# Tail of a decoder layer: one token tile finished on GpSimd, sums in column halves, the last tile read in halves

## The reference

```python
x = x + hybrid_mixer(rms_norm(x, norm1_w), ...)
x = x + hier_moe(rms_norm(x, norm2_w), ...)   # 32 experts, each token goes to 2
return rms_norm(x, final_norm_w)              # y * rsqrt(mean(y*y) + 1e-6) * w
```

## Time and profile before

| | us |
|---|---|
| median of 3 runs | 602.7 |
| profiled execution, its own time | 602.21 |
| span of that execution (first to last instruction) | 600.4 |
| scatter of pair 14, from its issue to its landing | 568.64 to 576.54 |
| last arithmetic instruction ends (VectorE, L2265) | 597.46 |

### The profile page before, as it was taken

The page is one execution under the profiler, slowest core; times in us unless marked ns, Lnnn a source line. Parts: engine busy times, 40 slices in busy tenths (PEclk is TensorE's granted clock), DMA queues, the critical chain, the costliest instruction groups (busy, mean ns, idle before and its releaser), DMA issues.

```text
span 600.4 us, 11954 instructions
## 1 busy us (share of the span) xinstructions
PE 573.6 (96%) x4899; PEld 441.8 (74%) x4899; DVE 252.5 (42%) x602; ACT 199.8 (33%) x429; POOL 182.9 (30%) x126
## 2 busy tenths in 40 slices
PE   8999999999999999999999999999999999987894
PEld 7978887999999888766789988656565656644541
DVE  6598534661138213465631073333222333221126
ACT  6656454723223352455525331111111211110113
POOL 3444443462557514323643202111121111210011
PEclk9999999999999999999999999999999999999998
DMA  8866543322211221004979787999999999999985
GB/s 335 330 210 194 151 146 106 105 73 73 71 38 37 72 71 37 1 2 162 408 255 411 274 320 261 396 426 426 424 426 426 426 425 424 422 427 427 413 325 221
DMA packets 32087, 152.73 MB, mean 254 GB/s; under 512 B 8759, under 2 KB 12511, under 8 KB 25376
## 3 DMA queue, kind: packets, MB, share of 16 engines
q1 hardware_dynamic: 27360, 143.77, 61.9%
q0 software_dynamic: 4528, 8.15, 3.6%
q10 hardware_dynamic: 144, 0.03, 0.0%
HBM read 143.78 MB, written 16.27 MB: 267 GB/s over the span
## 4 chain that ended last, share of the span: by engine, by line
PE 71%; DMA 19%; DVE 4%; issue 2%; POOL 1%; ACT 1%; POOLq 0%; SPq 0%; DVEq 0%; ACTq 0%
PE bank L796 32%; PE bank L843 11%; DMA xg<-h2d,tok 8%; DMA w<-in_expert_w_dram 8%; PE bank L1231 5%; PE bank L1190 4%; PE bank L1205 4%; PE bank L821 2%; PE bank L1129 2%; PE bank L1143 2%; DMA yd<-oy,dst 1%; PE bank L1123 1%; PE bank L1099 1%; PE bank L948 1%; PE bank L1015 1%
## 5 line engine op out<-in xcount | busy, mean ns | idle before, releaser
L1570 POOL TENSOR_TENSOR wlo<-raw,whi 128x1024 fp32r<-128x1024 f32 (+1 forms) x24 | 59.3, 2469 | 82.2 <-ACT whi L1260 78.8
L1697 POOL DMA_INDIRECT yd<-oy,dst x15 | 15.1, 1008 | 163.4 <-DVE oy L2226 152.7
L1190 PE MATMUL bank<-w,xT 128*64 128x256 f32 x512 | 58.2, 380 | 3.9 <-issue 3.9
L1205 PE MATMUL bank<-w,xT 128*64 128x256 f32 x512 | 58.1, 380 | 2.9 <-DMA w<-in_expert_w_dram 2.9
L1231 PE MATMUL bank<-w,hidT 128*64 128x512 f32 x256 | 58.5, 598 | 1.5 <-ACT hidT L1547 1.5
L1190 PEld LDWEIGHTS bank<-w,xT 128*64 128x64 f32 x512 | 37.4, 137 | 27.9 <-issue 12.5
L796 PE MATMUL bank<-wlo,hHi 128*128 128x256 f32 (+2 forms) x192 | 55.9, 291 | 0.0
L1205 PEld LDWEIGHTS bank<-w,xT 128*64 128x64 f32 x512 | 36.6, 137 | 21.8 <-DMA w<-in_expert_w_dram 3.8
L796 PE MATMUL bank<-whi,hHi 128*128 128x256 f32 (+1 forms) x176 | 50.6, 287 | 0.0
L2204 DVE SCALAR_TENSOR_TENSOR hid<-bank,slot,sa 128x256 f32<-128x256 f32 x16 | 10.8, 674 | 94.5 <-issue 91.9
L796 PE MATMUL bank<-whi,hLo 128*128 128x256 f32 (+1 forms) x176 | 49.6, 282 | 0.0
(11 more groups left out here) (385 smaller groups left out, 1167.7 us busy)
## 6 DMA issues: line engine op xcount, KB each, us to landing
w<-in_expert_w_dram SPq DMA_DIRECT2D x43, 2048.0 KB, 22.1
raw<-in_w_in_dram SPq DMA_DIRECT2D x24, 512.0 KB, 4.0
w<-in_expert_w_dram SPq DMA_DIRECT2D x10, 1024.0 KB, 7.2
yd<-zt SPq DMA_DIRECT2D x8, 512.0 KB, 5.1
yt<-yd SPq DMA_DIRECT2D x4, 1024.0 KB, 9.2
raw<-in_w_in_dram SPq DMA_DIRECT2D x6, 520.0 KB, 5.5
xt<-in_turned_dram SPq DMA_DIRECT2D x4, 512.0 KB, 6.7
X<-in_x_dram SPq DMA_DIRECT2D x4, 512.0 KB, 10.3
```

The lines of the kernel that those rows point to most:

```text
L1190: m = pe.matmul(pb[3][r, 0:FF], xT[:, c, r], w1[u % 4][:, e, c * FF:(c + 1) * FF], start=(c == 0), stop=(c == KC - 1), skip_group_check=True)
L1205: m = pe.matmul(pb[7][r, 0:FF], xT[:, c, r], w3[u % 4][:, e, c * FF:(c + 1) * FF], start=(c == 0), stop=(c == KC - 1), skip_group_check=True)
L1570: pool.tensor_tensor(low_of(g), raw_of(g), high_of(g).bitcast(F32), ALU.subtract).then_inc(wlo_done, 1)
L1697: pool.indirect_dma_start(yd.ap()[:, :], bass.IndirectOffsetOnAxis(ap=dst_i[o][:, 0:1].bitcast(U32), axis=0), oy[o][:, :], None, bounds_ch ...
```

## The change

Tile 1 is finished by GpSimd alone: after VectorE's add(1), GpSimd multiplies the tile by a copy of the norm row in SBUF (`fnb`, which ScalarE copies out of the two PSUM banks), and then by the reciprocal `rf`, in two halves. VectorE keeps only the reciprocal of tile 1 (`root(1)`). GpSimd's adds of the choices of tiles 0 and 1 come in column halves, each with its own count, and VectorE waits half by half. The last tile is read from `yd` in two column halves (`s_y[3]`, `s_last`), and TensorE counts each half of tiles 2 and 3. SP waits for tile 1's halves on `fin_pool`. TensorE's 8 norm-row products are spread: 3 where they all stood, 3 after the last up product, 2 after the turn of `hid`. Two semaphores are merged into others (`s_fn` into `s_rw`, `pool_step` into `pool_self`).

```diff
@@ sync
-            for t in range(T):
-                sp.dma_start(yt[t][:, :, :], yd.ap().rearrange("(k t p) d -> t p k d", k=2, p=P)[t]).then_inc(s_y[t], 16)
-            for t in range(T):
+            rows = yd.ap().rearrange("(k t p) d -> t p k d", k=2, p=P)
+            for t in range(T - 1):
+                sp.dma_start(yt[t][:, :, :], rows[t]).then_inc(s_y[t], 16)
+            sp.dma_start(yt[T - 1][:, :, 0:512], rows[T - 1][:, :, 0:512]).then_inc(s_y[T - 1], 16)
+            sp.dma_start(yt[T - 1][:, :, 512:D], rows[T - 1][:, :, 512:D]).then_inc(s_last, 16)
+            for t, done, count in ((0, fin_done, 0), (1, fin_pool, 0), (2, fin_done, 2), (3, fin_done, 4)):
                 for i in range(2):
-                    sp.wait_ge(fin_done, 2 * t + i + 1)
+                    sp.wait_ge(done, count + i + 1)
                     cs = slice(i * 512, (i + 1) * 512)
                     sp.dma_start(outv[t][:, cs], yt[t][:, 1, cs]).then_inc(s_out, 16)
@@ tensor, in unit(p, u) of the last pair
-                    pe.wait_ge(s_fn, 16)
-                    norm_rows(range(KC)).then_inc(fn_full, 1)
+                    pe.wait_ge(s_rw, 64)
+                    norm_rows(range(0, 3))
...
+                else:
+                    norm_rows(range(3, 6))
...
+                if u == PAIRS - 1:
+                    norm_rows(range(6, KC)).then_inc(fn_full, 1)
@@ tensor, tail
             for t in (2, 3):
-                pe.wait_ge(s_y[t], 16)
-                for i, b in enumerate(LAST[t]):
-                    m = pe.matmul(pb[b][:, :], ident, yt[t][:, 1, i * 512:(i + 1) * 512], start=False, stop=True)
-                m.then_inc(last_full, 1)
+                for i, (b, landed) in enumerate(zip(LAST[t], (s_y[t], s_last if t == 3 else s_y[t]))):
+                    pe.wait_ge(landed, 16)
+                    pe.matmul(pb[b][:, :], ident, yt[t][:, 1, i * 512:(i + 1) * 512], start=False, stop=True).then_inc(last_full, 1)
@@ scalar, tail
             act.activation(PDT[0:1, 0:1], eps[0:1, :], ACT.Sqrt)
+            act.wait_ge(fn_full, n)
+            for i, b in enumerate(FNB):
+                act.activation(fnb[:, i * 512:(i + 1) * 512], pb[b][:, :], ACT.Copy)
@@ gpsimd, tail
             for t in (0, 1):
                 pool.wait_ge(s_y[t], 16)
-                pool.tensor_tensor(yt[t][:, 0, :], yt[t][:, 0, :], yt[t][:, 1, :], ALU.add).then_inc(yy_done, 1)
+                for i in range(2):
+                    cs = slice(i * 512, (i + 1) * 512)
+                    pool.tensor_tensor(yt[t][:, 0, cs], yt[t][:, 0, cs], yt[t][:, 1, cs], ALU.add).then_inc(yy_done, 1)
+            pool.wait_ge(ssf_done, 1)
+            pool.wait_ge(acc_done, 2)
+            pool.tensor_tensor(yt[1][:, 1, :], yt[1][:, 0, :], fnb[:, :], ALU.mult).then_inc(yy_done, 1)
+            pool.wait_ge(yy_done, 5)
+            pool.wait_ge(rf_done, 2)
+            for i in range(2):
+                cs = slice(i * 512, (i + 1) * 512)
+                pool.tensor_tensor(yt[1][:, 1, cs], yt[1][:, 1, cs], rf[:, 1:2].broadcast_to([P, 512]), ALU.mult).then_inc(fin_pool, 1)
@@ vector, tail
-            dve.wait_ge(fn_full, 1)
-            def finish(t):
+            def root(t):
                 dve.wait_ge(ssf_done, 2 * t + 2)
                 dve.reciprocal(rf[:, t:t + 1], ssf[:, t:t + 1]).then_inc(rf_done, 1)
+            def finish(t):
+                root(t)
                 dve.wait_ge(rf_done, t + 1)
...
             for t in range(T):
-                if t < 2:
-                    dve.wait_ge(yy_done, t + 1)
-                else:
-                    dve.wait_ge(s_y[t], 16)
-                dve.wait_ge(last_full, t + 1)
                 for i, b in enumerate(LAST[t]):
+                    if t < 2:
+                        dve.wait_ge(yy_done, 2 * t + i + 1)
+                        dve.wait_ge(last_full, t + 1)
+                    else:
+                        dve.wait_ge(s_last if t == 3 and i else s_y[t], 16)
+                        dve.wait_ge(last_full, 2 * (t - 1) + i + 1)
                     cs = slice(i * 512, (i + 1) * 512)
                     j = dve.tensor_tensor(yt[t][:, 0, cs], pb[b][:, :], yt[t][:, 0, cs], ALU.add)
                 j.then_inc(acc_done, 1)
-                if t:
-                    finish(t - 1)
-            finish(T - 1)
+                if t == 1:
+                    finish(0)
+                if t == 2:
+                    root(1)
+            finish(2)
+            finish(3)
```

More of the change, by code:

```diff
@@ L516, in build @@
         selT = at("selT", [P, S], W1_AT[0] + 4 * KB)
+        fnb = at("fnb", [P, D], W1_AT[0] + 8 * KB)
         zt = at("zt", [P, D], R3 + 32 * KB)
@@ L545, in build @@
         sel_ready = sem("sel_ready"); idx_full = sem("idx_full"); idx_ready = sem("idx_ready"); gathered = [sem(f"gathered{i}") for i in range(3)]
-        xt_full = sem("xt_full"); xt_ready = sem("xt_ready"); up_full = sem("up_full"); gate_full = sem("gate_full"); sa_ready = sem("sa_ready"); loop_self = sem("loop_self"); next_rank = sem("next_rank"); pool_step = sem("pool_step")
+        xt_full = sem("xt_full"); xt_ready = sem("xt_ready"); up_full = sem("up_full"); gate_full = sem("gate_full"); sa_ready = sem("sa_ready"); loop_self = sem("loop_self"); next_rank = sem("next_rank");
         hid_ready = sem("hid_ready"); ht_full = sem("ht_full"); ht_ready = sem("ht_ready")
-        oyA = sem("oyA"); oyB = sem("oyB"); scattered = [sem(f"scattered{i}") for i in range(2)]; s_fn = sem("s_fn")
+        oyA = sem("oyA"); oyB = sem("oyB"); scattered = [sem(f"scattered{i}") for i in range(2)]
+        s_last = sem("s_last"); fin_pool = sem("fin_pool")
         s_y = [sem(f"s_y{t}") for t in range(T)]
@@ L716, in _ @@
             sp.dma_start(w1[3][:, 1, :], w1v[3][:, 1, :]).then_inc(w1_full[3], 16)
-            sp.dma_start(fnr[:, :], fnw.rearrange("(c p) -> c p", p=P)).then_inc(s_fn, 16)
+            sp.dma_start(fnr[:, :], fnw.rearrange("(c p) -> c p", p=P)).then_inc(s_rw, 16)
             sp.wait_ge(route_done, 1)
@@ L1549, in unit @@
                     turned(U + 1)
-            passes(act, unit, lambda p: turned(p * PAIRS))
+            n = passes(act, unit, lambda p: turned(p * PAIRS))
             act.activation(PDT[0:1, 0:1], eps[0:1, :], ACT.Sqrt)
+            act.wait_ge(fn_full, n)
+            for i, b in enumerate(FNB):
+                act.activation(fnb[:, i * 512:(i + 1) * 512], pb[b][:, :], ACT.Copy)
             for t in range(T):
@@ L1687, in gather @@
                 pool.wait_ge(idx_ready, U + ready)
-                pool.sem_inc(pool_step, 1)
+                pool.sem_inc(pool_self, 1)
                 pool.indirect_dma_start(xg[s][:, :], None, h2d.ap()[:, :],
```

## The result

The changed kernel takes 600.07 us (median of 6 runs, 599.7 to 600.79) against 602.72 us: ratio 0.9949, 95% interval 0.9936 to 0.9962. A second timing, with a copy of it, gave 0.9945 (0.9926 to 0.9964). The profiled executions differ by 602.21 - 600.03 = 2.2 us, the timed medians by 2.65, and the ratio stands for 3.1. So there are two questions: whether the tail did what was worked out, and where the 0.5 to 0.9 us beyond the profiled executions come from.

A forecast was written before the change was run, and what follows sets the result against it. The tail was taken as bound by tile 1's landing, GpSimd's add, VectorE's work, then the last tile's ScalarE round trip. 0.6 + 1.4 - 0.2 = 1.8 us off 602.21 gave 600.4, so 600.9 us median, range 600.1 to 602.1.

The forecast's parts named there:

- Adds in halves: Tail, add(1): VectorE adds the first half while GpSimd does the second, ending 0.6 us earlier (0.4 to 0.9).
- Tile 1's finish off VectorE: Tail, between add(2) and add(3): two multiplies leave VectorE's queue, gaining 1.4 us (1.3 if the reciprocal keeps its distance).
- Round trip over ScalarE: Tail, after add(3): ScalarE's square and root for tiles 2 and 3 become tighter, taking back 0.2 us.
- GpSimd: Tail, tile 1's multiplies on GpSimd: end near 593.5 and cost nothing, with cover of 0.9 us.
- the rival that GpSimd blocks VectorE: Tail: VectorE multiplies wait for GpSimd's instructions, net slower by 0.5 to 1.7 us, some 603.8 us; chance 0.04.
- Last tile in halves: Tail, tile 3's read: second half lands at 590.2 like the whole, up to 0.2 later, within a 0.3 margin.
- That rival: Tile 3's second half begins only when the first lands: 0.5 us slower, 603.2 us; chance 0.05.
- TensorE: the step that failed: Last pair and tail: TensorE, done at 592.22, is no bound; 1.3 us from spreading norm products is worth nothing.

The follow-up runs named there:

- e_halves: Kernel before with only GpSimd's adds of tiles 0 and 1 in column halves and VectorE waiting half by half: 603.02 us, ratio 0.9998.
- e_count: Kernel before with semaphore merges and only the counting by halves of tiles 2 and 3, last tile read whole: 602.24 us, ratio 0.9974.
- e_read: Kernel before with semaphore merges and only the last tile read in two DMAs, counting as before: 603.48 us, ratio 0.9996.
- e_last2: Repeat of the kernel before with semaphore merges, last tile read in halves and halves counted: 601.83 us, ratio 0.9972.
- a_nonorm: Changed kernel with all 8 norm-row products together again ahead of the last gate product: 600.57 us, ratio 0.9951 to the kernel before.
- b_copy: Kernel before, unchanged, as a control: 603.34 us, ratio 0.9996.
- b_keep: Kernel before with 9 small filler products ahead of each wait for weights in pairs 13 and 14: 602.85 us, ratio 1.0001.
- e_last: Kernel before with semaphore merges, last tile read in halves and halves counted, first timing: 601.65 us, ratio 0.9971.
- e_pool: Kernel before with semaphore merges, the norm-row copy and tile 1 finished by GpSimd alone: 601.21 us, ratio 0.9970.

## Why the prediction was wrong, point by point

*Adds in halves.* Forecast 0.6. From tile 1's landing to the end of add(1) (8.2 us after an issue at 576.98, so 585.18; now 8.0 after 576.81, 584.81) it was 588.90 - 585.18 = 3.72, and it is now 588.08 - 584.81 = 3.27: 0.45. A half costs 1.25, near the upper of the two neighbouring rows (1.27), so the lower gain, 0.4, was the right one. What the prediction did not see is that this gain needs an earlier bank from TensorE: alone it was lost to TensorE at once in e_halves' profile. In the changed kernel both the spread norm rows and the counting by halves give that; which of them is needed isn't shown.

*Tile 1's finish off VectorE.* Forecast 1.4. From add(1)'s end to add(3)'s end 594.31 - 588.90 = 5.41, now 592.05 - 588.08 = 3.97: 1.44.

*Round trip over ScalarE.* Forecast 0.2 back. From add(3)'s end to VectorE's end 3.15, now 3.40: 0.25 back. Add to this that the reads started 0.18 earlier and tile 1 landed some 0.2 sooner after that, and 0.45 + 1.44 - 0.25 + 0.37 gives the 2.0 by which VectorE ends earlier. So the change itself made 1.64 in this pair of executions, a little less than the forecast's 1.8, and 0.37 of the 2.0 is luck, that of two executions that differ in their DMAs. The landing differs from execution to execution, in kernels with the same reads too: in the 20 profiles of this study tile 1 lands 7.2 to 8.3 us after its issue.

*GpSimd.* Forecast to end near 593.5, measured 593.05. The two halves with the broadcast reciprocal took 1.04 each, not 1.18. VectorE beside it kept its times (two multiplies 1.41 from 588.19, with GpSimd busy from 588.23), so the rival that GpSimd blocks VectorE is out.

*Last tile in halves.* The halves overlap: they landed at 588.6 and 590.0, where the whole had landed at 590.2. That rival is out as well. Alone the read in halves is worth nothing that can be measured; with the rest of the change it may be worth 0.6 to 0.8 us, with overlapping intervals.

*TensorE: the step that failed.* TensorE "is done at 592.22 and is not the bound", says the prediction, and of TensorE's 1.3 us "It is worth nothing". So its sum has no term for TensorE, and above all none for handing over the banks of tiles 2 and 3 one by one. That hand-over alone measured 0.26% (e_count, 1.6 us), and a microsecond of TensorE's work more costs the kernel before 2 us. The reading was right for the one execution that it was taken from, at 602.21 us with a mean clock of 0.996, where TensorE is 0.3 ahead at add(2) (590.00 against 590.32). It fails where the last gate product takes 5.36 us (e_read, VectorE's end 1.5 later) and where tile 1 lands after 7.2 to 7.3 us (e_last2, e_count). The prediction carried the gain of the profiled execution over to the median, 603.3 us over 132 runs, as a constant.

How much of what is missing this accounts for stays open. At a mean clock of 0.996 or more the kernel before averages 602.4 us (20 runs) and the changed kernel 600.0 (9 of its 12 runs): a gain of 2.4, close to the 2.2 of the profiled executions. So of the 3.1 us some 0.7 go with the lower clock of the other runs, by association and not by experiment. Of the counting's 1.6 us the profiles show at most 0.9 on VectorE, in a dip, and 0.5 in the landing of the last write, without a cause. The intervals of the single edits, 0.1 to 0.2% to either side, do not allow the parts to be added up to the 3.1 us. For the place of the 1.3 us itself the prediction may have been right: spreading the norm rows has no clear effect of its own (0.9989, up to 1.0001, and 0.06% in a_nonorm).

## What to carry to other kernels

Where two engines hand each other the last tiles, a slack of 0.3 us in one profiled execution is no slack: look at the spread of the timed runs, at their mean clock and at when the loads land in other profiles, and ask which engine would come last if TensorE were 1 to 2 us later. Handing over by halves paid here, although the profile of before shows no wait. A gain at one wait holds only if the next engine in line is early too, so try such edits together as well as one by one. And where an edit measures more than its mechanism can give, as the counting did, say so, and take profiles of several executions before it is called explained. Moving an elementwise finish to an idle GpSimd paid (0.30% alone) although it takes three times as long there (4.4 us against 1.41), as long as its writes do not bunch up ahead of the last ones.

## What was not expected of the hardware

- The last pair's gate product, 32 products of 128x256, took 3.67 us at a granted clock of 1.0 and 5.36 us where the grant fell to a mean of 0.57 to 0.63 over 4 us, right behind 16 to 24 small norm-row instructions and without a wait of TensorE in front. The same 5.36 us stands in pair 14's gate product of six profiles, where no norm rows precede it (in b_copy at 551.57, after 2.03 us in which TensorE did nothing).
- Runs with four norm products more have a mean clock of 0.9902, the kernel before 0.9929, that with three of the eight in that place 0.9956. Other kernels with all eight there lie at 0.9927 to 0.9949 (b_keep, with its fillers, at 0.9950), so the last step is not clear.
- Time from the last write's issue to its landing varied from 2.0 to 3.2 us between kernels with the same last instructions (2.5 in before, 3.2 in e_halves, 2.0 in e_last, e_last2, e_count and e_pool).
- The second of four 1 MB reads issued together landed 7.2 to 8.3 us after its issue, over the 20 profiles.
- Five writes of 256 KB in a row took 0.48 us each to issue, against 0.33 for a single one of before.
